# A decoder block with product-key experts on one Trainium2 core: fourth head's query weights loaded during routing, four down rows, small sums for the first eight experts, query copies ahead of exponentials, another routing order

## The reference

```
def peer_ffn(h, w_q, sub_keys, u_table, v_table):      # n = 256 tokens
    q = (xt @ w_q).reshape(n, 8, 2, 128)                # 8 heads, 2 sides
    s = einsum('nhpc,pkc->nhpk', q, sub_keys)           # 128 keys a side
    sv, si = top_k(s, 16)
    cand = sv[..., 0, :, None] + sv[..., 1, None, :]    # 16 x 16 sums
    top_s, pos = top_k(cand, 16)
    experts = side index 0 * 128 + side index 1, at pos
    gates = softmax(top_s)
    act = gelu(x . u_table[expert]) * gates             # 16 per head and token
    out = sum over 8 x 16 experts of act * v_table[expert]
```

## Time and profile before

| what | value |
|---|---|
| median of three runs | 2417.31 us |
| the profiled execution, its own time | 2416.0 us |
| its span, first to last instruction | 2414.1 us |
| mean granted clock of TensorE in it | 0.989 |
| busy: TensorE / VectorE / ScalarE / GpSimd | 2150.4 / 1529.0 / 684.0 / 669.2 us |
| read from HBM over the span | 703.63 MB |

### The profile page before, as it was taken

The page is one execution under the profiler, slowest core; times in us unless marked ns, Lnnn a source line. Parts: engine busy times, 40 slices in busy tenths (PEclk is TensorE's granted clock), DMA queues, the critical chain, the costliest instruction groups (busy, mean ns, idle before and its releaser), DMA issues.

```text
span 2414.1 us, 37754 instructions
## 1 busy us (share of the span) xinstructions
PE 2150.4 (89%) x15287; PEld 1508.2 (62%) x15287; DVE 1529.0 (63%) x2602; ACT 684.0 (28%) x1366; POOL 669.2 (28%) x539
## 2 busy tenths in 40 slices
PE   7999999999999999998988998978887787777776
PEld 7999999999899999987644444433332332222222
DVE  7778888888765555548776577667445444444445
ACT  6555555455344444432211111111011000000000
POOL 1000000000000000004654554655455445444442
PEclk9999999999999999999999999999999999999999
DMA  6433333333367666677999999999999999999997
GB/s 206 137 97 102 104 88 98 102 89 100 106 184 193 186 188 185 194 261 301 414 423 425 423 427 426 427 427 427 427 427 426 426 427 427 427 427 427 427 427 297
DMA packets 346273, 708.19 MB, mean 293 GB/s; under 512 B 13835, under 2 KB 270435, under 8 KB 279779
## 3 DMA queue, kind: packets, MB, share of 16 engines
q0 software_dynamic: 74176, 537.01, 52.8%
q1 hardware_dynamic: 271684, 168.55, 23.9%
q10 hardware_dynamic: 240, 0.22, 0.0%
HBM read 703.63 MB, written 2.10 MB: 292 GB/s over the span
## 4 chain that ended last, share of the span: by engine, by line
DMA 33%; PE 16%; DVE 4%; issue 2%; POOL 2%; DVEq 1%; ACT 0%; POOLq 0%; ACTq 0%
DMA down_rows<-in_v_table,experts 17%; DMA rows<-in_v_table,experts 8%; PE bank L1899 7%; DMA rows<-in_u_table,experts 5%; PE project L1899 3%; DMA up_rows<-in_u_table,experts 3%; PE bank L232 2%; PE bank L1815 1%; DVE rows L2009 1%; PE project L232 1%; POOL down_rows L1780 1%; POOL rows L1780 0%; PE bank L1842 0%; PE bank L1857 0%; POOL rows L1774 0%
## 5 line engine op out<-in xcount | busy, mean ns | idle before, releaser
L2009 DVE CUSTOM_DVE_ANT_0 rows<-rows,h 128x2048 f32<-128x2048 f32 x170 | 389.0, 2291 | 338.7 <-DMA rows<-in_u_table,experts 338.7
L1899 PE MATMUL bank<-down_rows,diagonal 128*128 128x512 f32 x908 | 423.2, 602 | 86.4 <-DMA down_rows<-in_v_table,experts 67.3
L1774 POOL DMA_INDIRECT rows<-in_u_table,experts x170 | 188.4, 1108 | 1122.6 <-DVE experts L1416 1045.5
L1899 PEld LDWEIGHTS bank<-down_rows,diagonal 128*128 128x128 f32 x908 | 167.1, 190 | 329.9 <-issue 182.8
L217 DVE TENSOR_TENSOR w_half_rest<-w_half,w_half_high 128x1024 fp32r<-128x1024 f32 x224 | 271.3, 1219 | 160.5 <-ACT w_half_high L196 160.3
L232 PE MATMUL project<-hT_high,w_half_high 128*128 128x272 f32 (+1 forms) x1152 | 351.1, 305 | 0.4 <-PEq L239 0.3
L1899 PE MATMUL bank<-rows,diagonal 128*128 128x512 f32 x612 | 286.9, 606 | 54.9 <-DMA rows<-in_v_table,experts 41.5
L232 PE MATMUL project<-hT,w_half_high 128*128 128x272 f32 (+1 forms) x1152 | 329.3, 286 | 0.0
L232 PE MATMUL project<-hT_high,w_half_rest 128*128 128x272 f32 (+1 forms) x1152 | 328.8, 285 | 0.0
L2009 DVE CUSTOM_DVE_ANT_0 up_rows<-up_rows,h 128x2048 f32<-128x2048 f32 x86 | 196.9, 2291 | 177.0 <-DMA up_rows<-in_u_table,experts 177.0
L1780 POOL DMA_INDIRECT down_rows<-in_v_table,experts x153 | 221.3, 1446 | 297.9 <-PE bank L1899 289.5
(11 more groups left out here) (413 smaller groups left out, 3516.8 us busy)
## 6 DMA issues: line engine op xcount, KB each, us to landing
w_half<-in_w_in SPq DMA_DIRECT2D x176, 512.0 KB, 4.2
w_half<-in_w_branch_a SPq DMA_DIRECT2D x32, 512.0 KB, 4.0
out_w<-in_w_out SPq DMA_DIRECT2D x16, 1024.0 KB, 5.5
query_w<-in_w_q_peer SPq DMA_DIRECT2D x10, 1024.0 KB, 21.3
w_half<-in_w_branch_b SPq DMA_DIRECT2D x16, 512.0 KB, 4.0
out_w<-in_w_q_peer SPq DMA_DIRECT2D x6, 1024.0 KB, 25.3
lora_weights<-in_w_in SPq DMA_DIRECT2D x4, 896.0 KB, 14.0
rows<-in_u_table,experts POOLq DMA_INDIRECT x170, 21.1
```

The source lines that it names most:

```text
L1774: pool.indirect_dma_start(ur[n % RU], None, w["u_table"][0], bass.IndirectOffsetOnAxis(ap=k.idx[:, t, h, j:j + 1], axis=0)).then_inc(s_u[n ...
L1899: mm = nc.tensor.matmul(acc[t][c][:], dg[n % RD][:], vr[n % RV][:, quarter(c)], start=(n == 0), stop=(n == last(t, c)), skip_group_check=True)
L2009: v.tensor_tensor_reduce(ur[n % RU], ur[n % RU], k.h[:, n // (HEADS * TOPK), :], 1.0, 0.0, ALU.mult, ALU.add, dots[:, n:n + 1]).then_inc(s ...
```

## The change

Query weights get four homes; head 3 goes to the first tile's half of the buffers `mergedT` and `mergedT_high`, which are no longer read once tile 0's product is done. Its two loads (512-byte pieces, 1 MB each) are issued there. The two down rows beyond the first two now lie in head 0's query weights; diagonals, dots and weights lie in the second tile's half of the merged buffers. `RV` goes from 5 to 4, and two down gathers are issued at first, the next two after `up(8)`, when head 0's queries are made. The first eight experts come from the best eight of either side (8 x 8 sums, one-hot rows of 8). Two dots go ahead of the second tile's norm. The order of the routing becomes (0,0), (1,0), (0,1), (1,1), then as before, and semaphore values follow by `routed`. Head 2's scores are made after unit 2. Cut to its core:

```diff
+QUERY_HOME = (0, 1, 2, 3, 1, 2, 1, 2)
+ROUTED = {(1, 0): 2, (0, 1): 3}
...
+        self.spare = [self.over(f"merged_spare{i}", [P, KT, SEQ], self.merged_at + 4 * KT * SEQ * i) for i in range(2)]
...
     def load_query(self, eng, w, h, i):
+        home, c0 = QUERY_HOME[h], h * 2 * P
+        if home == 3:
+            dst, src = self.spare[i][:, :, 0:P], src[:, :, c0 + i * P:c0 + (i + 1) * P]
...
+def routed(h, t):
+    return ROUTED.get((h, t), 2 * h + t + 1)
...
+def route_halves(k, dve, h, t):
+    v, d = k.nc.vector, k.nc.vector.drain
+    sv, si, sif, tv, ti = k.sv, k.si, k.sif, k.tv, k.ti
+    best, rest, n = slice(0, 8), slice(8, 16), 8
+    flat = k.cand[:].rearrange("p a b -> p (a b)")
+    block = flat[:, 0:n * n]
+    dve.wait_ge(k.s_s, 2 * h + t + 1)
+    for i in range(2):
+        v.max(sv[:, i, best], k.sc[:, t, i, :])
+    d()
+    pairs(k, block, n)
+    for i in range(2):
+        v.max_index(si[:, i, best], sv[:, i, best], k.sc[:, t, i, :])
+    d()
+    v.max(tv[:, best], block)
+    v.tensor_copy(sif[:, :, best], si[:, :, best])
+    d()
+    v.max_index(ti[:, best], tv[:, best], block)
+    d()
+    experts(k, h, t, best, n).then_inc(k.s_ahead, 1)
+    for i in range(2):
+        v.match_replace(k.sc2[:, i, :], sv[:, i, best], k.sc[:, t, i, :], -3.0e38)
...
+    pairs(k, flat, TOPK)
...
+    experts(k, h, t, rest).then_inc(k.s_idx, 1)
...
                 k.load_query(sp, w, 1, i)
+            sp.wait_ge(s_mm, TT * (NB - 1) + 1)
+            for i in range(2):
+                k.load_query(sp, w, 3, i)
...
-    RV, RD, UNIT = 5, 8, 4
+    RV, RD, UNIT = 4, 8, 4
+    FIRST_DOWN, EARLY = 2, 2
...
-            for h in range(3, HEADS):
-                sp.wait_ge(s_qmm, 2 * (h - 3) + 2)
+            for h in range(4, HEADS):
+                sp.wait_ge(s_qmm, 2 * max(g for g in range(h) if QUERY_HOME[g] == QUERY_HOME[h]) + 2)
...
-            for n in range(RV):
+            for n in range(FIRST_DOWN):
                 down(n)
...
                         up(n)
+                        if n == TOPK // 2:
+                            pool.wait_ge(s_qmm, 2)
+                            for m in range(FIRST_DOWN, RV):
+                                down(m)
...
-                if r == 0 and 2 <= h + AHEAD < HEADS:
+                if u == 2:
+                    score(2)
+                if r == 0 and 3 <= h + AHEAD < HEADS:
                     score(h + AHEAD)
...
             for u in range(UNITS):
                 g, r = divmod(u, PER_HEAD)
-                if u == 1:
-                    exps(k, act, 0, 1)
-                if r > 1 and g + 1 < HEADS:
+                if r == 2 and g + 2 < HEADS:
+                    query(g + 2)
+                if r > 1 and g + 1 < HEADS and u != 3:
                     exps(k, act, g + 1, r - 2)
                 if 1 <= u <= CLOSER:
                     diagonal(u - 1)
-                if r == 2 and g + 2 < HEADS:
-                    query(g + 2)
...
                 if u == 0:
                     query(1)
                     scores(1, 0)
+                if u == 2:
                     scores(1, 1)
+                    exps(k, act, 0, 1)
...
                 if r == 3 and g + 2 < HEADS:
                     scores(g + 2, 0)
                     scores(g + 2, 1)
+                if u == 3:
+                    exps(k, act, 1, 1)
...
+            dve.wait_ge(k.s_out_mm, OUT_MM)
+            for n in range(EARLY):
+                dot(n)
             x = k.h[:, 1, quarter(3)]
-            dve.wait_ge(k.s_out_mm, OUT_MM)
             residual(k, x, late[3][:])
...
-                if u == 0:
-                    route(k, dve, 0, 1)
-                if u == 1:
-                    gate(0, 1)
                 if g + 1 < HEADS:
                     if r == 1:
                         route(k, dve, g + 1, 0)
                     if r == 2:
                         gate(g + 1, 0)
-                        route(k, dve, g + 1, 1)
+                        route(k, dve, g + 1 if g else 0, 1)
                     if r == 3:
+                        if g == 0:
+                            gate(0, 1)
+                            route(k, dve, 1, 1)
                         gate(g + 1, 1)
```

More of the change, by code:

```diff
@@ L1416, in experts, with pairs, route @@
     return v.tensor_copy(k.idx[:, t, h, j], ex)
-def route(k, dve, h, t, halves=False):
+def pairs(k, out, n):
+    return k.nc.vector.tensor_tensor(out.rearrange("p (a b) -> p a b", b=n),
+                                     k.sv[:, 0, 0:n].rearrange("p (a b) -> p a b", b=1).to_broadcast((P, n, n)),
+                                     k.sv[:, 1, 0:n].rearrange("p (a b) -> p a b", a=1).to_broadcast((P, n, n)), ALU.add)
+def route_halves(k, dve, h, t):
[20 more added lines that the diff above has]
+        v.match_replace(k.sc2[:, i, :], sv[:, i, best], k.sc[:, t, i, :], -3.0e38)
+    d()
+    for i in range(2):
+        v.max(sv[:, i, rest], k.sc2[:, i, :])
+    d()
+    pairs(k, flat, TOPK)
+    for i in range(2):
+        v.max_index(si[:, i, rest], sv[:, i, rest], k.sc2[:, i, :])
+    d()
+    v.tensor_copy(sif[:, :, rest], si[:, :, rest]).then_inc(k.s_scored, 1)
+    v.match_replace(k.cand2[:], tv[:, best], flat, -3.0e38)
+    d()
+    v.max(tv[:, rest], k.cand2[:])
+    d()
+    v.max_index(ti[:, rest], tv[:, rest], k.cand2[:])
+    v.tensor_tensor(k.gates[:, t, h, :], tv[:], tv[:, 0:1].to_broadcast((P, TOPK)), ALU.subtract).then_inc(k.s_shift, 1)
+    d()
+    experts(k, h, t, rest).then_inc(k.s_idx, 1)
+def route(k, dve, h, t):
     v, d = k.nc.vector, k.nc.vector.drain
@@ L1428, in route @@
     d()
[L1429 to L1443, removed]
+    flat = cand[:].rearrange("p a b -> p (a b)")
     best16(v, lambda _: tv[:], lambda _: ti[:], lambda _: flat, lambda _: k.cand2[:], range(1))
@@ L1712, in route_peer_stage, with of @@
         ur = [k.up_row(i) for i in range(RU)]
-        rows_at = -(-k.merged_at // ROW_ALIGN) * ROW_ALIGN
-        vr = [k.rows[:, 4 + i, :] for i in range(2)] + [k.over(f"down_rows{2 + i}", [P, D], rows_at + 4 * D * i)[:] for i in range(RV - 2)]
-        small = rows_at + 4 * D * (RV - 2)
-        dg = [k.over(f"diagonal{i}", [P, P], small + 512 * i) for i in range(RD)]
-        dots, weights = k.over("dots", [P, SLOTS], small + 4096), k.over("weights", [P, SLOTS], small + 5120)
-        aid, pick = k.over("alpha_identity", [P, P], small + 6144), k.over("row_of_two", [2, 2, P], small + 6656)
+        flat = k.first_query[:].rearrange("p k c -> p (k c)")
+        vr = [k.rows[:, 4 + i, :] for i in range(FIRST_DOWN)] + [flat[:, D * i:D * (i + 1)] for i in range(RV - FIRST_DOWN)]
+        high, low = (x[:, :, P:SEQ] for x in k.spare)
+        dg = [high[:, i, :] for i in range(RD)]
+        aid, pick = low[:, 4, :], low[0:2, 5:7, :]
+        def of(first, n0, n1):
+            t, j = divmod(n0, P)
+            return low[:, first + t, j:j + n1 - n0]
+        dots, weights = (lambda n0, n1: of(0, n0, n1)), (lambda n0, n1: of(2, n0, n1))
         gam, bet, stats, mv, rs = k.gam, k.bet, k.stats, k.mv, k.rs
@@ L2014, in weigh @@
                 dve.wait_ge(s_gelu, u + 1)
-                dve.wait_ge(s_gate, 2 * h + t + 1)
-                v.tensor_tensor(weights[:, UNIT * u:UNIT * (u + 1)], dots[:, UNIT * u:UNIT * (u + 1)], k.gates[:, t, h, j:j + UNIT],
+                dve.wait_ge(s_gate, routed(h, t))
+                v.tensor_tensor(weights(UNIT * u, UNIT * (u + 1)), dots(UNIT * u, UNIT * (u + 1)), k.gates[:, t, h, j:j + UNIT],
                                 ALU.mult).then_inc(s_weight, 1)
```

66 lines of the change are left out of this document (37 added, 29 removed).

## The result

The changed kernel takes 2421.91 us (median of 14 runs, 2418.40 to 2423.73), the kernel before 2415.68 (14 runs, 2413.43 to 2417.95): ratio 1.0024, 95% interval 1.0017 to 1.0031. The forecast was 4.3 us more than before, the runs show 6.2 (4.1 to 7.5). The profiled execution has a span of 2420.2 us (before: 2414.1), its own time is 2421.99, the granted clock 0.991.

What follows compares the result with a forecast made beforehand. DMA gathers bound the kernel: their start and the queue's dry spells set the end. U22 +4.1, head 5's load -0.3, end +0.5 give +4.3 us: 2421.6 us; own range 2419 to 2426, with rivals 2410 to 2431.

Steps and rivals of the forecast that it cites:

- two waits in series: VectorE's gates of head 1's two tiles wait for ScalarE's exponentials, behind copies needing TensorE after slots 3 and 11.
- U0 issued: First up gather, issued by GpSimd at 1097.8 us instead of 1101.12, 3.3 us earlier through small sums.
- slot 0: TensorE's slot 0 begins at 1137.4 us instead of 1140.53, taken as warm.
- dot 16 starts: VectorE's dot 16, behind the gate of head 1's second tile, starts at 1207.9 us; before, it ran at 1185.35.
- U22 lands: Up gather 22, the 37th gather, lands at 1217.0 us instead of 1212.9: +4.1 us.
- the second wait: gate(1,1) and dot 16 wait for exponentials behind copies of head 2's scores, made after slot 11; dry spell of 10.2 us.
- rival A: Waits stay hidden: dot 16 ends by about 1199, no second dry spell, -5.7 us, 2411.6 us; chance 0.20.
- cold slot 4: TensorE idles 2.5 us before slot 4; a cold spell there up to +2 us, held only in the range.
- After U22: TensorE at 4.6 us per slot keeps ahead of the DMA (4.91), all goes on as before; end +0.5 us.
- rival B: From 1217 us on, four down rows too few: 2445 us at landing limit 16.1, 2428 at 15.7; chance 0.13.
- real but spent in waiting: Earlier first gather (3.3 us) and head 3's weights moved before the gathers (6.0 us) are spent in the second dry spell.
- the first dry spell: Ten gathers last until 1125.5 us, U8 lands at about 1131, so the queue runs dry for 3 us.

Runs made afterwards that it cites:

- experiment 1: Changed kernel with ScalarE's exponentials of head 1, second tile, moved ahead of its copies of head 2's scores: 2411.15 us, ratio to before 0.998.
- experiment 4: Changed kernel with TensorE computing head 2's scores after slot 7 (unit 1) in place of slot 11, ScalarE's order kept: 2411.84 us.
- experiment 8: Kernel of experiment 1 with no dots ahead of the second norm (`EARLY` 0 instead of 2): 2413.53 us.
- experiment 9: Kernel of experiment 1 with dot 2 between third and fourth part of the second norm, two small constants built after the first four dots: 2412.09 us.
- experiment 5: Kernel before the change with four buffers for down rows in place of five, nothing else: 2416.58 us, ratio 1.0005.
- experiment 7: Kernel before the change with only the small sums for the first eight experts added: 2415.12 us, ratio 0.9996.
- experiment 6: Kernel of experiment 1 with head 3's weights loaded back in the full stretch, where the kernel before loads them: 2418.38 us, ratio 1.0009.
- experiment 10: Kernel of experiment 9 with down rows 2 and 3 issued behind up row 9 in place of up row 8: 2412.11 us.
- experiment 2: Kernel of experiment 1 with, in unit 2, head 2's query copies also moved behind head 1's first-tile exponentials and diagonals: 2411.90 us, ratio 0.9984.

## Why the prediction was right, point by point

The forecast, with its two waits in series, held. That 2421.6 us came within 0.3 us of the measured 2421.91 is luck: it stood on a median before of 2417.31 us, from three runs, which fourteen put at 2415.68, and its increase was 1.9 us too small; the two errors cancel. In the times of before (1.96 us added):

| step | predicted | measured |
|---|---|---|
| U0 issued | 1097.8 | 1097.98 |
| slot 0 | 1137.4 | 1136.92 |
| slot 4 | 1167.4 | 1167.08 |
| dot 16 starts | 1207.9 | 1209.43 |
| U22 lands | 1217.0 | 1219.4 |

- **The path, both waits.** Right in place, order and releaser. Experiments 1 and 4 take the second wait away from either end and give 2411.15 and 2411.84; rival A had put the kernel without the dry spell at 5.7 us below before, 2411.6; measured were 4.6.
- **U22's landing, 2.4 us too early in the sum.** Two terms. The cold slot 4 that the sum left out, and only the range held, happened in this trace: TensorE was idle for 2.37 us and the window 1165 to 1170 follows at a lower granted clock (0.66, between the two levels); slot 4 took 5.20 us until the next product instead of 3.44, +1.8. The same pause of 2.37 us is followed by a slot 4 at the full clock in the traces of experiments 4, 8 and 9, so the term comes in some executions and not in others. And the landing was 7.4 us, the upper of the two figures that the sum lay between, not 6.6: +0.8. The Trainium skill, "SBUF — State Buffer", section "Who interferes with whom", has a VectorE instruction with two SBUF inputs block only GpSimd's reads; from that the prediction worked out descriptors that are not late and a landing at 1216.0. The trace does not bear this conclusion out: the issue beside the dots took 2.82 us instead of 1.01, and the landing came 7.4 us behind its start instead of 5.6, later by as much. Whether the gather's own reading of its expert numbers is what is held up, which would fit the rule, no run here shows.
- **After U22, +0.2 predicted, +1.5 measured** (1217.4 to the landing of the last down row, 2406.83, is 1189.4 us; before, 1212.89 to 2400.79 is 1187.9). The four rows are not free. What the prediction missed stands at 1736 to 1760. TensorE spreads gamma and beta of the last layer norm with eight matmuls of two rows, and towards their end its granted clock falls to half, 1.2 GHz, and stays there behind them:

```profile
1736.88 4.33 PE L1925 MATMUL bank<-query_w,merged_spare 2*128 2x512 f32 x8
1741.14 3.78 PE L1967 MATMUL project<-rows,merged_spare 128*128 128x512 f32 x4
1744.71 2.84 PE L1967 MATMUL bank<-rows,merged_spare 128*128 128x512 f32 x4
```

```profile
1740.00:1745.00 5.00, 5.00 (x7) 1.79 (x6) 2.30 (x2) 0.00 (x0) 0.05 (x1) 0.50 1.01 426
1745.00:1750.00 5.00, 5.00 (x11) 2.06 (x11) 2.30 (x2) 0.00 (x0) 1.87 (x2) 0.84 1.04 419
1750.00:1755.00 5.00, 5.00 (x13) 2.25 (x12) 2.30 (x2) 0.21 (x1) 3.18 (x3) 1.00 0.98 397
1755.00:1760.00 5.00, 5.00 (x12) 2.01 (x11) 2.37 (x3) 1.28 (x4) 4.04 (x4) 1.00 0.96 365
```

GpSimd waits 7.78 us for a down buffer (issue at 1747.83), and the DMA engines run at 397 and 365 GB/s: (427 - 397) x 5 + (427 - 365) x 5 = 460 kB, 1.1 us.

```profile
1747.83 0.93 POOL L1844 DMA_INDIRECT rows<-in_v_table,experts  x1 [7.78 <-PE bank L1967]
```

Before, with five rows, the clock fell to 0.52 in the same place, and no window was below 423:

```profile
1735.00:1740.00 5.00, 5.00 (x7) 1.85 (x6) 2.30 (x2) 0.00 (x0) 0.18 (x1) 0.52 1.02 429
1740.00:1745.00 5.00, 5.00 (x10) 2.00 (x9) 2.30 (x2) 0.00 (x0) 1.75 (x2) 0.79 1.02 431
1745.00:1750.00 5.00, 5.00 (x13) 2.28 (x12) 2.30 (x2) 0.20 (x1) 3.31 (x3) 1.00 1.00 423
1750.00:1755.00 5.00, 5.00 (x12) 2.01 (x11) 2.37 (x3) 1.28 (x4) 4.01 (x3) 1.00 1.01 426
```

So rival B was right in a small form: a fifth row does not raise the rate, it covers one late TensorE. Other executions with four rows show such a gap too (experiment 5 above, 310 GB/s in the window 1660 to 1670 of experiment 4, 344 in that of experiment 9), the two with five rows (before and experiment 7) don't. No run has five rows with the rest of the change, since no room was found for a fifth, so its price of about 1 us is read from traces and bounded by experiment 5 (0.8 us, not told from zero), not shown by taking it away. One sum of the rival was off as well: by its own formula a landing limit of 15.7 us makes a slot 4.925 us long, 3 us over 200 slots and 2424.6 us, not a quarter of 24 us and 2428.
- **The two together.** 4.3 + 2.4 + 1.3 = 8.0 us, and from the routing's start to the end this pair of traces differs by 8.1 (2420.2 - 1090.42 against 2414.1 - 1092.38). The medians differ by 6.2: this execution made up 2 us ahead of the routing. In the traces of all ten experiments the stretch from the routing's start to the end differs from before by what the medians say, within 0.6 us; here it is 1.9 us longer. So this was a long stretch for the kernel. A slot 4 at the lower clock, 1.8 us, would explain it, but only one trace of the changed kernel exists and this stays open. The sizes of single terms are good to a microsecond or two, no better.
- **Early gathers and moved load "real but spent in waiting".** The moved load is worth 7.2 us (6.0 predicted) where the DMA is full behind it (experiment 6). The 3.3 us of the small sums (3.1 measured) are worth 1.0 +- 2.2 in the kernel before (experiment 7): there too most is spent in waiting, but in another place, which the prediction did not look for.
- **Early dots and the first dry spell.** U8 was issued at 1122.90 and landed 6.8 us later, in the times of before at 1131.7 (predicted 1131), and the gap is near the 3 us worked out: shares 0.64 and 0.80. Experiments 8 to 10 moved the dots and the down gathers in three ways and won nothing (0.9 to 2.4 us more, which intervals of +- 2.2 us hardly tell from zero). My reading is that the gap stays as long as VectorE has the norm and the dots to do in the same 20 us; no run shows that, and nothing else was tried to close it.

The best version found is that of experiment 1: 2411.15 us, faster than before by 0.11 to 0.29% and than the changed kernel by 10.8 us; experiments 2, 4, 9 and 10, at 2411.8 to 2412.1, can't be told from it.

## What to carry to other kernels

Where transfers fill the run, count transfers and not waits: a wait costs what it makes the queue run dry, and its end counts, not its length. An 11 us wait cost nothing that the runs can tell next to a full queue (experiment 2), and one of 12 us cost 10.8. When a producer's copy is moved ahead of a small instruction that another engine waits for, look at when the copy's input is ready; here two lines of order turned a gain of 4.6 us into a loss of 6.2. A gain at the start of a stream has to be followed to every later point where the stream can run dry.

## What the runs showed of the hardware that was not expected

- TensorE's granted clock fell to 0.50 of full speed, 1.2 GHz, in the window 1740 to 1745 with the engine busy for all 5 us; ahead of it stood eight matmuls with two rows of weights (4.33 us), and ahead of these some 3.8 of each 5 us busy. It is not the rule: behind the same eight matmuls, in experiment 9 at 1728.05, the granted clock stayed at 1.00. Ahead of slot 4 the same idleness of 2.4 us was followed by 0.66 in the changed kernel and by 1.00 in experiments 4, 8 and 9. Idleness of 5.95 us stood ahead of slot 12 (0.73 and 0.58 in the windows from 1205 to 1215).
- Two loads of one megabyte in 512-byte pieces, put on SyncE's queue beside a full queue of gathers, took 36.6 us to land and cost the run 7.2 us, near the 6.0 us of their share. The short pieces are not what makes it long: later query weights of the changed kernel, in pieces of 1024 bytes, took 36.2 us.
- The landing of one gather on an empty queue is 5.6 us with an issue of 1.01 us (U0), 6.8 with one of 2.24 us (U8) and 7.4 with one of 2.82 us (U22), the last two beside VectorE's dots.
